# Retention kernel: the last projection further behind its heads, the work of a head spread out, and sample states stored from SyncE

## The chip, the cores and the metric

One core of a Trainium2 chip runs the whole program. The metric is the device time of one execution in microseconds (us). TensorE multiplies, VectorE (DVE) and ScalarE (ACT) work element by element, GpSimd (POOL) does a few operations, and SyncE (SP) issues most of the DMA transfers; ScalarE issues the rest. Each engine takes its instructions strictly in the order of the program, and the engines wait for each other on semaphores.

## What is computed

One inference step of a two-layer decoder for 512 prompt tokens and 8 x 8 sample tokens, 576 in all, in float32. Layer 0 is differential attention; the change starts where it ends. Layer 1 is multi-scale retention:

```python
for layer in range(DEPTH):
    ...
        hp = rms_norm(y_prompt, norm_pre_ret)
        hs = rms_norm(y_sample, norm_pre_ret)
        qp, kp, vp, gp = ret_project(hp, w_in_ret, pos_prompt)      # 2048 -> 12288
        op, sp = retention_prompt(qp, kp, vp, log_g)                # chunks of 128 tokens, 8 heads
        ss, osm = retention_chunk(state_ret, qs, ks_, vs, log_g)    # 8 samples, state (256, 512) per head
        y_prompt = y_prompt + rms_norm(ret_output(op, gp, w_out_ret), norm_post_ret)
        ret_state_sample = ss
...
def ret_output(o, g, w_out):
    on = head_rms_norm(o)...
    return (on * jax.nn.silu(g)) @ w_out                            # 4096 -> 2048
```

The states of the samples are read and written: 8 samples x 8 heads x 512 KB each way.

## The kernel before

The kernel is a list of stages in one order, written by a planner at build time; each engine goes through the whole list and does its share of each stage. The clock of the list is the **tile** (a **slot**): one `project` stage, six matmuls of 128x288. A large matrix product in float32 is made of three products of halves: every operand is split into a high part (`WH`, `XH`, made by ScalarE's copy, L1531) and a residue (`WL`, `XL`, made by VectorE's subtraction, L1845 for weights and L1850 for tokens). A weight chunk of 512 KB (`WR`) serves eight tiles; at the third tile of each chunk the next one is split and the one three further on is loaded (`load_w`, L1100).

Behind layer 0 come three stages of the program.

*Between the layers* (`norm_between`): the norms, and beside them the first input projections of layer 1 as tiles. Four quarters of the tokens are put together again from `XH` and `XL` (`x_rec`, 128x2304 each, two on VectorE L2110 and two on GpSimd L2370), mixed (`x_mix`, L2116) and split (`x_mix_split`, L2121), for the products that follow.

*The products* (`layer_one_inputs`): 42 of the 48 column blocks (head, kind) of the input projection, each in seven products of half size (24 matmuls of 128x288 each) where plain tiles need 32 tiles of six. The results go to `retention_inputs` in memory.

*The last stage* (`layer_one`): it lays the retention of eight heads under a stream of tiles. `retention_work` gives each head a table of slots, 64 slots per head (`PER_HEAD`). The stream begins with the three column blocks of head 7 that are left (96 tiles, `FILL`), and then come eight **parts** of the output projection, 64 tiles each: part h multiplies the gated tokens of head h. So part h begins at slot 96 of head h's own count. A head's stages, by name:

- `load_v4`, `load_qk`, `load_g4`: its inputs; `natural` (`r`): transposes of the values through bank 7, copied by ScalarE; `rope`: four VectorE operations per input (L2137 to L2142).
- `rs_keys`, `pad_rows`, `rs_mask`, `rs_out`, `rs_state`: the samples. `rs_out` is 17 matmuls of 128x512 (34 records); `rs_state` adds the new keys to the eight states in four steps of four banks (4 to 7), each drained by VectorE (L2207).
- `ret_scores`, `ret_out`, `ret_state` for four chunks; `ret_rstd` and `ret_norm` (L2199); `gate`: transposes, multiplied by VectorE with the gate (L2220).
- `store_ret` writes the gated tokens to memory (`gated_retention`), `load_x` (L1106) reads them back into `XL`, and four `split_x` (ScalarE L1531, VectorE L1850) make them ready for the part.
- `load_state` and `store_state` move the eight states, 512 KB each. A load waits until the store of the same buffer (head before) has landed.

The order in which a head's stages stand around the next head's is set by that table alone:

```python
    def put(t, *s):
        at.setdefault(max(t, -PER_HEAD * h), []).extend(s)
```

`store_state` waits for banks 4 to 7 to be drained and is issued by ScalarE (L1749). `load_x` waits for the stores of the gated tokens and for the matmuls before it.

## Time and profile before

| | before |
|---|---|
| median of 3 runs | 3733.25 us (3732.2 to 3734.78) |
| profiled execution | 3740.97 us, its span 3739.0 us |
| TensorE busy | 3418.2 us, 91% |
| VectorE busy | 2207.4 us, 59% |
| ScalarE busy | 1097.9 us, 29% |
| GpSimd busy | 87.4 us, 2% |
| read and written | 593.36 MB and 98.96 MB |

By the trace the stage between the layers lies from about 1600 to 1768 us, the products from there to about 2700 us, and the last stage from there to the end. Busy shares are means over stages with different limits; a matmul in the records is pipelined, so that a busy TensorE can still be one at half its clock. The row PEclk and the column PEclk give the clock that was granted.

### The profile page before, as it was taken

How to read it: one execution, taken by the hardware profiler on the slowest of the kernel's cores; microseconds unless marked ns; L12 is line 12 of the kernel's file. 1: busy time of each engine (PE TensorE's matmuls, PEld its weight loads, DVE VectorE, ACT ScalarE, POOL GpSimd, SP SyncE). 2: the span in 40 equal slices, each digit the busy share in tenths (PEclk: the TensorE clock that was granted, in tenths of full speed). 3: DMA queues.
4: the chain of work that ended last, by engine and by line, in shares of the span. 5: the costliest groups of instructions: out<-in, count | busy, mean ns of one | idle time of the engine just before them, and what ended most of it. 6: DMA issues, size and time to landing. Idle time of an engine off the chain costs nothing.

```text
span 3739.0 us, 65337 instructions
## 1 busy us (share of the span) xinstructions
PE 3418.2 (91%) x25236; PEld 3003.2 (80%) x25236; DVE 2207.4 (59%) x3329; ACT 1097.9 (29%) x1604; POOL 87.4 (2%) x89
## 2 busy tenths in 40 slices
PE   7999999999999998888999999999988778887787
PEld 7988887788788776778999999999976656666567
DVE  4466656565656664375777767777643455545555
ACT  4223222222222322143333333333323311222213
POOL 1000000000000000030000000000000000000000
PEclk9999999999999998999999999999999989998899
DMA  5466887788788877534333333333345554455534
GB/s 176 155 209 214 273 283 254 262 287 278 243 281 273 276 261 243 184 130 138 116 116 129 126 122 116 116 131 124 126 155 204 180 187 149 142 182 177 181 121 147
DMA packets 497127, 698.18 MB, mean 187 GB/s; under 512 B 37042, under 2 KB 295219, under 8 KB 493683
## 3 DMA queue, kind: packets, MB, share of 16 engines
q1 hardware_dynamic: 419010, 593.18, 48.0%
q10 hardware_dynamic: 77392, 100.55, 7.7%
q8 instruction: 201, 3.29, 0.4%
q0 software_dynamic: 416, 0.28, 0.1%
q14 instruction: 108, 0.88, 0.1%
HBM read 593.36 MB, written 98.96 MB: 185 GB/s over the span
## 4 chain that ended last, share of the span: by engine, by line
PE 76%; DVE 10%; DMA 5%; issue 3%; ACT 3%; SPq 1%; ACTq 0%; DVEq 0%; POOL 0%; POOLq 0%
PE low_banks L1227 49%; PE high_banks L1227 25%; DMA XL<-gated_retention 3%; PE high_banks L1230 2%; DVE area L2207 2%; DVE WL L1845 2%; DMA area<-in_cache_v 1%; ACT WH L1531 1%; DVE x_rows L1867 1%; DVE area L1941 1%; SPq L1132 1%; DVE area L2142 1%; ACT area L1531 0%; DVE area L2140 0%; DVE XL L1850 0%
## 5 line engine op out<-in xcount | busy, mean ns | idle before, releaser
L1227 PE MATMUL low_banks<-XH,WH 128*128 128x288 f32 (+2 forms) x4528 | 1127.9, 316 | 134.7 <-DVE XL L1850 87.8
L1227 PE MATMUL low_banks<-XH,WL 128*128 128x288 f32 (+2 forms) x4528 | 1055.0, 300 | 0.0
L1227 PE MATMUL low_banks<-XL,WH 128*128 128x288 f32 (+2 forms) x4528 | 1053.7, 299 | 0.0
L1227 PEld LDWEIGHTS low_banks<-XH,WH 128*128 128x128 f32 x4528 | 766.2, 193 | 298.2 <-issue 166.3
L1227 PEld LDWEIGHTS low_banks<-XL,WH 128*128 128x128 f32 x4528 | 769.3, 193 | 0.0
L1227 PEld LDWEIGHTS low_banks<-XH,WL 128*128 128x128 f32 x4528 | 768.6, 193 | 0.0
L1227 PE MATMUL high_banks<-area 128*32 128x256 f32 (+9 forms) x4720 | 650.2, 477 | 57.3 <-DVE area L2220 16.3
L1227 PEld LDWEIGHTS high_banks<-area 128*32 128x32 f32 (+3 forms) x4720 | 279.3, 142 | 277.1 <-issue 204.4
L1845 DVE TENSOR_TENSOR WL<-WR,WH 128x1024 fp32r<-128x1024 f32 x266 | 330.3, 1242 | 283.2 <-ACT WH L1531 277.9
L1531 ACT ACTIVATE WH<-WR 128x1024 fp32r<-128x1024 f32 x266 | 280.8, 1056 | 544.2 <-PE low_banks L1227 400.3
L1941 DVE STREAM_TRANSPOSE area<-area 128x512 f32<-128x512 f32 x512 | 334.7, 691 | 106.6 <-PE high_banks L1227 63.9
L1531 ACT ACTIVATE area<-high_banks 128x512 f32<-128x512 f32 (+2 forms) x224 | 118.7, 535 | 819.8 <-PE high_banks L1230 482.0
L2081 DVE TENSOR_TENSOR WL<-area,WH 128x1024 fp32r<-128x1024 f32 x196 | 240.2, 1226 | 154.0 <-ACT WH L1531 151.6
L1531 ACT ACTIVATE WH<-area 128x1024 fp32r<-128x1024 f32 x196 | 208.5, 1064 | 267.2 <-DVE area L2075 163.6
L1230 PE MATMUL high_banks<-eye_sb,area 128*128 128x128 f32 (+2 forms) x984 | 162.2, 286 | 104.6 <-DVE area L2199 45.0
L2075 DVE TENSOR_TENSOR area<-area 128x1024 f32<-128x1024 f32 x168 | 205.9, 1226 | 23.8 <-DVE third L2081 1.0
L1230 PEld LDWEIGHTS high_banks<-eye_sb,area 128*128 128x128 f32 (+2 forms) x984 | 117.3, 145 | 127.6 <-issue 63.5
L1227 PE MATMUL low_banks<-mixes,WH 128*128 128x288 f32 x896 | 178.9, 294 | 0.0
L1227 PE MATMUL high_banks<-mixes,WH 128*128 128x288 f32 x896 | 178.9, 294 | 0.0
L2081 DVE TENSOR_TENSOR third<-area,third 128x1024 fp32r<-128x1024 f32 x98 | 120.1, 1226 | 93.6 <-ACT third L1531 92.7
L1531 ACT ACTIVATE third<-area 128x1024 fp32r<-128x1024 f32 x98 | 104.3, 1064 | 158.3 <-DVE area L2075 83.1
L1227 PEld LDWEIGHTS low_banks<-mixes,WH 128*128 128x128 f32 x896 | 144.6, 189 | 0.0
(178 smaller groups left out, 3153.1 us busy)
## 6 DMA issues: line engine op xcount, KB each, us to landing
area<-in_cache_k SPq DMA_DIRECT2D x512, 256.0 KB, 4.6
area<-in_cache_v SPq DMA_DIRECT2D x512, 256.0 KB, 5.2
area<-in_w_in_ret SPq DMA_DIRECT2D x168, 512.0 KB, 5.8
WR<-in_w_in_attn SPq DMA_DIRECT2D x136, 512.0 KB, 5.3
out<-area ACTq DMA_DIRECT2D x73, 512.0 KB, 4.0
WR<-in_w_out_ret SPq DMA_DIRECT2D x66, 512.0 KB, 3.5
area<-in_state_ret SPq DMA_DIRECT2D x64, 512.0 KB, 10.8
retention_inputs<-area ACTq DMA_DIRECT2D x48, 576.0 KB, 2.9
```

Of the source, the lines that this page charges most:

```text
L1132: sp.dma_start(Vr[t:128:GROUP, half * GROUP:(half + 1) * GROUP, :], cv[page, :, pair * 512:(pair + 1) * 512].rearrange("a (o j) n -> j (a ...
L1227: return nc.tensor.matmul(out, a, b, start=start, stop=stop, skip_group_check=True)
L1230: return nc.tensor.matmul(out, a, ident[0:n, 0:n], start=True, stop=True, is_transpose=True, skip_group_check=True)
L1531: return nc.scalar.activation(out, in_, ACT.Copy, scale=scale)
L1845: v.tensor_tensor(WL[:, slot, :, :], WR[:, slot, :, :], WH[:, slot, :, :].bitcast(f32), SUB).then_inc(sem["w_lo"], 1)
L1867: last = v.tensor_tensor(dst[:, lo:hi], bank[2 * cb + b][:, 0:hi - lo], dst[:, lo:hi], ADD)
L1941: v.transpose(KTs[:, :, 128 * (u % 2) + 32 * pp:128 * (u % 2) + 32 * pp + 32], Kr[:, slot, :].rearrange("p (m i) -> p m i", i=32)).then_in ...
L2075: v.tensor_tensor(to, a, b, op).then_inc(sem["quad_sums"], 1)
L2081: v.tensor_tensor(lo, quad(r, what), hi.bitcast(f32), SUB).then_inc(sem["w_lo"], 1)
L2142: v.tensor_tensor(mine[:], mine[:], rt[:], ADD).then_inc(sem["rotated"], 1)
L2207: v.scalar_tensor_tensor(out=mine, in0=mine, scalar=decay8[:, g:g + 1], in1=bank[4 + j][:, :], op0=MUL, op1=ADD).then_inc(sem[f"drained{4 ...
```

## The change

It has five parts.

1. *Distance.* `FILL` goes from 96 to 128 and every head's table moves by `BASE` = 8. Part h now begins 120 slots behind the start of head h's table, where it was 96. The 32 tiles that fill the gap are two column blocks that leave the products: (0,3) goes to the stage between the layers and (7,2) to the last stage (40 blocks remain in the products, and 656 tiles stand in the last stage where there were 624).
2. *Spread.* Within a head's table `load_x` goes from slot 72 to 84 and `split_x` from 78, 80, 82, 84 to 105, 109, 113, 117; `load_state` from every 2 slots at 6 to every 3 at 22 (slots of the next head); `rs_out` from 49 to 56; `rs_state` from 56, 59, 62, 65 to 65, 69, 73, 77; the gates from 52, 55, 58, 61, 64 to 54, 57, 60, 63, 67.
3. *Stores.* `store_state` is issued by SyncE, two slots apart from slot 73 on (61 before).
4. *Between the layers.* All four `x_rec` go to GpSimd, one behind the other; the mixes and their splits go in halves of 128x1152 into slots 133 to 191, where the tiles of (0,2) and (0,3) run.
5. *Slots of weights.* The products' ring begins at slot 0, and the first weight chunk of the last stage is loaded into `spare_chunk`, the room of the products' `first_sum`, one product earlier than before.

```diff
-FILL = 96
+FILL = 128
 PER_HEAD = 64
+BASE = 8
...
     def put(t, *s):
-        at.setdefault(max(t, -PER_HEAD * h), []).extend(s)
+        at.setdefault(max(BASE + t, -PER_HEAD * h), []).extend(s)
...
-            put(6 + 2 * k + (2 if k > 3 else 0), Stage("load_state", b=2 * (k % 4) + k // 4))
+            put(22 + 3 * k, Stage("load_state", b=2 * (k % 4) + k // 4))
...
-        put(52 + 3 * t, Stage("gate", t=t))
-        put(54 + 3 * t, Stage("store_ret", t=t))
...
+        put(54 + 3 * t, Stage("gate", t=t))
+        put(57 + 3 * t, Stage("store_ret", t=t))
+    put(56, Stage("rs_out"))
...
-            put(56 + 3 * (2 * g + e), Stage("rs_state", g_=g, e=e))
+            put(65 + 4 * (2 * g + e), Stage("rs_state", g_=g, e=e))
         for j in range(4):
-            put(61 + 7 * g + 2 * j, Stage("store_state", b=2 * j + g))
-    if h < HEADS:
-        kt = CH * (h % 2)
-        put(72, Stage("load_x", part=h % 2, kt=kt, row=CH * h, width=T, layer=1))
-        for k in range(CH):
-            put(78 + 2 * k, Stage("split_x", part=h % 2, kt=kt + k, width=T))
+            put(73 + 8 * g + 2 * j, Stage("store_state", b=2 * j + g))
+    kt = CH * (h % 2)
+    put(96 if h == 0 else 84, Stage("load_x", part=h % 2, kt=kt, row=CH * h, width=T, layer=1))
+    for k in range(CH):
+        put(105 + 4 * k, Stage("split_x", part=h % 2, kt=kt + k, width=T))
...
-          24: lambda: n.scale(4), 25: lambda: rec((0, 0), 2, "pool"), 26: lambda: rec((1, 0), 4, "pool"),
-          36: lambda: n.transpose(4), 40: lambda: rec((1, 1), 3, "dve"), 46: lambda: rec((0, 1), 1, "dve"), 52: lambda: mix(3),
...
+          24: lambda: n.scale(4), 36: lambda: n.transpose(4), 40: lambda: rec((0, 0), 2) + rec((1, 0), 4) + rec((1, 1), 3) + rec((0, 1), 1),
...
-    order = [(n, (n, lo, hi)) for lo, hi in ((0, EARLY), (EARLY, T)) for n in range(2)] + [(2, None)]
+    order = [(n, (n, lo, hi)) for lo, hi in ((0, EARLY), (EARLY, T)) for n in range(2)] + [(2, None), (3, None)]
...
-    for s in range(3, 6):
+    for s in range(2, 6):
...
-    todo = [(h, s) for h in range(HEADS) for s in range(6)][3:-3]
+    todo = [(h, s) for h in range(HEADS) for s in range(6)][4:-4]
...
+            def store_state(g, b):
+                for n in range(4, 8):
+                    sp.wait_ge(sem[f"drained{n}"], c.before(f"drained{n}"))
+                sp.dma_start(st_out[g + b * HEADS], Sin[:, b, :].rearrange("p (e v) -> p e v", e=2)).then_inc(sem[f"state_out{b}"], 16)
```

In the order of the changed program line numbers are a few off: L1103 is `load_w`, L1109 `load_x`, L1202 `load_state`, L1207 `store_state`, L1195 `load_g4`, L1188 `load_v4`, L1235 a matmul and L1238 a transpose, L1849 the subtraction for `WL`, L2286 that for `XL` in the norm, L2111 a mix and L2365 a sum on GpSimd.

**SyncE, from one head's `load_g4` to the loads of the next head's states.** Before:

```order
L1199 DMA area<-in_state_ret 128x2x512
L1192 DMA area<-retention_inputs 128x4x576
L1106 DMA XL<-gated_retention 128x4x576
L1199 DMA area<-in_state_ret 128x2x512 x2
L1100 DMA WR<-in_w_out_ret 128x4x256
L1199 DMA area<-in_state_ret 128x2x512 x3
```

Of the change:

```order
L1207 DMA out<-area 128x2x512
L1195 DMA area<-retention_inputs 128x4x576
L1103 DMA WR<-in_w_out_ret 128x4x256
L1207 DMA out<-area 128x2x512 x4
L1103 DMA WR<-in_w_out_ret 128x4x256
L1207 DMA out<-area 128x2x512
L1109 DMA XL<-gated_retention 128x4x576
L1207 DMA out<-area 128x2x512
L1202 DMA area<-in_state_ret 128x2x512
L1207 DMA out<-area 128x2x512
L1188 DMA area<-retention_inputs 128x4x576
L1202 DMA area<-in_state_ret 128x2x512
```

The load of `XL` stood among the loads of states; it now stands ahead of them, behind six stores.

**TensorE, at the third `rs_state` of a head.** Before, after two tiles of the projection, the transposes of the last gate and of the first `natural` follow (x8):

```order
L1227 MATMUL high_banks<-area 128x512 x4
L1227 MATMUL low_banks<-XH,WH 128x288 x2
L1227 MATMUL low_banks<-XL,WH 128x288 x2
L1227 MATMUL low_banks<-XH,WL 128x288 x2
...
L1230 MATMUL high_banks<-eye_sb,area 128x128 x8
```

Of the change, at the second and the fourth `rs_state`:

```order
L1235 MATMUL high_banks<-area 128x512 x4
L1238 MATMUL high_banks<-eye_sb,area 128x128 x4
L1235 MATMUL low_banks<-XH,WH 128x288 x2
...
L1235 MATMUL high_banks<-area 128x512 x4
L1235 MATMUL high_banks<-area 64x64 x2
L1238 MATMUL high_banks<-eye_sb,area 64x128 x2
```

A `natural` of the next head (`eye_sb`, 128x128) now stands directly behind the second `rs_state` (and one behind the third), and the matmuls of `rs_keys` (64x64) behind the fourth, with no tile between.

**VectorE, between the layers.** Before (L1845 is `WL`, L2110 a sum, L2116 a mix, L2290 the residues of the last tokens):

```order
L1845 TENSOR_TENSOR WL<-WR,WH 128x1024 x2
L2290 TENSOR_TENSOR XL<-high_banks,XH 128x4x64 x4
L2110 TENSOR_TENSOR area<-XH,XL 128x2304
L1845 TENSOR_TENSOR WL<-WR,WH 128x1024
L2110 TENSOR_TENSOR area<-XH,XL 128x2304
L1845 TENSOR_TENSOR WL<-WR,WH 128x1024
L2116 TENSOR_TENSOR area<-area 128x2304 x2
```

Of the change:

```order
L1849 TENSOR_TENSOR WL<-WR,WH 128x1024 x2
L2286 TENSOR_TENSOR XL<-high_banks,XH 128x4x64 x4
L1849 TENSOR_TENSOR WL<-WR,WH 128x1024 x12
L2111 TENSOR_TENSOR area<-area 128x1152 x2
```

The sums have left VectorE; twelve weight subtractions now follow one another before the first mix. On GpSimd the two sums are four.

## Rows read from the trace of the kernel before

**Rows 1.** The page, busy tenths and granted clock in 40 slices of the span.

```profile
PE   7999999999999998888999999999988778887787
...
PEclk9999999999999998999999999999999989998899
```

**Rows 2.** Stages: us, busy of PE, PEld, DVE, ACT, POOL; PEclk, DMA share, GB/s.

```profile
2400.00:2600.00 200.00, 200.00 (x1514) 200.00 (x1513) 141.93 (x144) 73.83 (x81) 0.00 (x0) 1.00 0.36 122
3050.60:3166.40 115.80, 93.11 (x555) 72.45 (x554) 60.51 (x98) 24.42 (x39) 2.62 (x2) 0.90 0.49 167
```

**Rows 3.** TensorE's waits, 2690 to 3739: us in total, times, longest.

```profile
PE low_banks L1227 <- DVE XL L1850: 79.0, 8, 10.7
PE high_banks L1230 <- DVE area L2199: 45.0, 24, 2.9
PE high_banks L1230 <- DVE area L2207: 22.1, 19, 2.0
PE high_banks L1227 <- DVE area L2220: 16.3, 21, 1.6
PE high_banks L1230 <- ACT area L1531: 9.9, 6, 6.7
PE high_banks L1227 <- DVE area L2161: 5.5, 8, 1.1
PE high_banks L1227 <- ACT area L1531: 5.4, 7, 1.7
```

**Rows 4.** The chain that ended last: start, us, what (longest and shortest of eight).

```profile
3398.04 15.58 DMA XL<-gated_retention
...
3618.26 11.98 DMA XL<-gated_retention
```

**Rows 5.** Timeline of one head: start, us, engine, line, operation, idle before.

```profile
3050.65 0.46 SPq L1106 DMA_DIRECT2D XL<-gated_retention  x1
...
3065.47 0.68 ACT L1531 ACTIVATE XH<-XL 128x576 fp32r<-128x576 f32 x1 [10.95 <-DMA XL<-gated_retention]
...
3069.04 0.85 PE L1227 MATMUL low_banks<-XH,WH 128*128 128x288 f32 x2 [10.23 <-DVE XL L1850]
...
3069.69 0.68 PE L1227 MATMUL low_banks<-XL,WH 128*128 128x288 f32 x2
...
3076.49 0.42 PE L1227 MATMUL low_banks<-XL,WH 128*128 128x288 f32 x2
```

**Rows 6.** The chain in the products stage: start, us, what.

```profile
1813.08 25.39 PE low_banks L1227 x192
```

**Rows 7.** DMA issues, 2830 to 3500: count, size, median us to landing.

```profile
WR<-in_w_out_ret SPq DMA_DIRECT2D x47, 512.0 KB, 3.5
...
area<-in_state_ret SPq DMA_DIRECT2D x45, 512.0 KB, 10.9
...
XL<-gated_retention SPq DMA_DIRECT2D x5, 1152.0 KB, 15.3
```

**Rows 8.** Timeline of the same head, from `rs_out` to the last `rs_state`.

```profile
3115.82 4.70 PE L1227 MATMUL high_banks<-area 64*128 64x512 f32 x34
...
3122.88 1.23 DVE L1845 TENSOR_TENSOR WL<-WR,WH 128x1024 fp32r<-128x1024 f32 x1 [6.28 <-ACT WH L1531]
...
3124.68 0.66 PE L1230 MATMUL high_banks<-eye_sb,area 128*128 128x128 f32 x4 [1.58 <-DVE area L2199]
...
3155.84 2.72 DVE L2207 SCALAR_TENSOR_TENSOR area<-area,high_banks 128x512 f32<-128x512 f32 x4 [1.81 <-PE high_banks L1227]
...
3158.71 0.63 PE L1230 MATMUL high_banks<-eye_sb,area 128*128 128x128 f32 x4 [1.97 <-DVE area L2207]
```

**Rows 9.** Between the layers: TensorE's waits for `WL`; timeline of GpSimd and VectorE.

```profile
PE low_banks L1227 <- DVE WL L1845: 23.1, 6, 6.0
...
1669.01 13.10 POOL L2370 TENSOR_TENSOR area<-XH,XL 128x2304 f32<-128x2304 f32 x2 [3.94 <-DVE XL L2290]
...
1671.10 12.09 DVE L1845 TENSOR_TENSOR WL<-WR,WH 128x1024 fp32r<-128x1024 f32 x2
```

More of the change, by code:

```diff
@@ L512, in split @@
         n, i = divmod(m, 7)
-        self.splits[m] = Stage("quad_split", r=n % 2, what=PRODUCTS[i], slot=(m + 2) % 3, summed=self.sums.get((n, PRODUCTS[i])))
+        self.splits[m] = Stage("quad_split", r=n % 2, what=PRODUCTS[i], slot=m % 3, summed=self.sums.get((n, PRODUCTS[i])))
         out = [self.splits[m]]
@@ L547, in layer_one_inputs @@
     for m in range(prods.count):
-        out += prods.split(m + 2) + prods.product(m) + after.get(prods.count - m, [])
+        out += (prods.split(m + 2) if m else []) + prods.product(m) + after.get(prods.count - m, [])
     return out + prods.store(len(prods.pairs) - 1)
@@ L577, in retention_work @@
             put(5 * hh + 2 * j, Stage("natural", what="r", hh=hh, j=j))
-    put(7, loads["g"])
-    put(20, Stage("silu_g"))
-    put(12, Stage("rs_keys"))
-    put(13, Stage("pad_rows"))
-    put(21, Stage("rs_mask"))
-    for c in range(4):
-        put(14 + 9 * c, Stage("ret_scores", c=c))
-        put(17 + 9 * c, Stage("ret_out", c=c))
-        put(18 + 9 * c, Stage("ret_state", c=c))
-    put(48, Stage("store_state_p"))
-    put(47, Stage("ret_rstd", t=0, n=4))
-    put(49, Stage("rs_out"))
@@ L590, in retention_work @@
-    put(54, Stage("ret_rstd", t=4, n=1))
-    for t in range(4):
-        put(50 + t, Stage("ret_norm", t=t))
-        put(52 + 3 * t, Stage("gate", t=t))
-        put(54 + 3 * t, Stage("store_ret", t=t))
-    put(57, Stage("ret_norm", t=4))
-    put(64, Stage("gate", t=4))
-    put(66, Stage("store_ret", t=4))
+    put(10, loads["g"])
+    put(24, Stage("silu_g"))
+    put(13, Stage("rs_keys"))
+    put(14, Stage("pad_rows"))
+    put(22, Stage("rs_mask"))
+    for c in range(4):
+        put(15 + 9 * c, Stage("ret_scores", c=c))
+        put(18 + 9 * c, Stage("ret_out", c=c))
+        put(19 + 9 * c, Stage("ret_state", c=c))
@@ L810, in plan @@
     stored = Stored(proj, prods, last)
-    begun = last.load(0) + last.load(1)
-    for x in begun:
-        x.a["behind_products"] = True
-    opening = {9: [Stage("load_rope")], 3: begun}
+    begun = last.load(0), last.load(1)
+    begun[0][0].a["spare"] = begun[1][0].a["behind_products"] = True
+    opening = {9: [Stage("load_rope")], 4: begun[0], 2: begun[1]}
     inputs = layer_one_inputs(prods, opening)
@@ L819, in plan @@
     at = inputs.index(prods.mm[prods.count - 1])
-    inputs[at:at] = [Stage("split_w", slot=0)] + last.load(2)
+    inputs[at:at] = [Stage("split_w", slot=1, spare=True)] + last.load(2)
     inputs += [Stage("relay_area"), Stage("pads"), Stage("load_head")] + [Stage("load_state", b=2 * (k % 4) + k // 4) for k in range(8)]
```

102 lines of the change are left out of this document (52 added, 50 removed).

## The prediction

> **What bounds the kernel now.** I began with the page's slices: TensorE is the engine that the time is made of, and in the last third its digit drops from 9 to 7 or 8 while its granted clock drops too [rows 1]. The table by stages says how much. In 200 us of the products stage TensorE is busy for all 200 us at clock 1.00; in one head of the last stage (115.8 us) it is busy for 93.1 us at clock 0.90 [rows 2]. A reader should see that an edit in the products stage could at best trade one TensorE instruction for another, and that some 25 us of each head are there to be won. So I asked for TensorE's waits from 2690 us to the end [rows 3]: 79.0 us in 8 waits are for `XL` (the residues of the gated tokens that a part multiplies), 45.0 us for `ret_norm` on VectorE (L2199), and 22.1 + 16.3 + 9.9 + 5.4 + 5.5 = 59.2 us for banks and operands that VectorE or ScalarE had still to drain or make.
>
> The chain shows what stands behind the 79 us: a load of `gated_retention` once per head, from 12.0 to 15.6 us each, eight of them [rows 4]. The timeline of one head has the story in order [rows 5]: SyncE issues the load at 3050.65; ScalarE, which takes its work in order, sits 10.95 us at the first `split_x`; VectorE follows; TensorE stands until 3069.04. After that its pairs of matmuls take 0.68 us and not 0.42, until about 3075.8, a little before the last row of the group. That is 6.8 us at the half clock (1.2 GHz), so 3.4 us lost on top of every 10 us wait.
>
> **Extra work.** Columns (0,3) and (7,2) leave the seven products and are computed tile by tile: 192 matmuls in place of 168, twice, at 25.39/192 = 0.132 us [rows 6]: **+6.3 us**. One tile (6 matmuls, a slot) is 0.79 us. Nothing hides this; TensorE is full there.
>
> **The load of XL.** Before, it is put at slot 72 of its head, its first split at 78 and the part at 96. Now they are at 84, 105 and 120 after the head's own start (each 8 later in the program's count). The load takes 15.3 us to land [rows 7]; 21 slots are 16.7 us of projection alone, and two chunks of retention lie between. It is also issued before the eight state loads rather than among them. The last split (slot 117) has 3 slots, 2.4 us, and the 4.7 us of `rs_out` [rows 8] in front of its user, against 0.68 us of work on ScalarE [rows 5] and about as much on VectorE. I take all 79 us and the 8 x 3.4 us: **-106 us**. Bounds: -40 (half of each wait returns, and the clock with it) and -106.
>
> **Gates.** Today `rs_out` and the weight split stand before three of the four `ret_norm`s on VectorE: it idles 6.28 us for `WH`, and the gate waits 1.58 us [rows 8]. Now `rs_out` comes 7 slots later, behind the norms. But `rope` and now a `split_x` lie among the norms, so I keep one wait of 2.5 us per head (between today's mean, 1.9, and longest, 2.9): 45 becomes 20, **-25 us**. Bounds 0 and -45.
>
> **Banks.** Here the change costs. `rs_state` moves from slots 56, 59, 62, 65 to 65, 69, 73, 77, straight into the next head's `natural` (64, 66, 68, 69, 71, 73, all bank 7) and `rs_keys` (77). VectorE drains an `rs_state` in 2.72 us, bank 7 last; the one natural that stands a slot behind one today waits 1.97 us [rows 8]. Per head: natural behind gate 3 on bank 7, 1.6 (today's longest L2220 wait [rows 3]); natural 66, 2.0; naturals 69 and 73 with no slot between, 2.7 and 2.3; `rs_keys` 0.8 until bank 4 is free; `ret_scores` 0 two slots later needs bank 4 again, after 2.72 and the operations of `rs_keys` ahead of it, the largest on 1024 elements like a `WL` (1.23, [rows 8]), 2.1; ScalarE's drains 1.0. That is 12.5 us, and for seven heads and a rest of 4 us some 91 us, against 52.5 us today (59.2 less the 6.7 us of the start). **+39 us**, and **+5 us** for more time at the half clock in so broken a stretch. Bounds: 0, and +112 (TensorE and VectorE take turns wholly, about 20 us per head).
>
> **Between the layers.** The four half-size sums of `XH` and `XL` now all go to GpSimd, and the eight mixes to slots where nothing is short. Today two sums on GpSimd take 13.10 us, 6.55 each, and in that time VectorE's two `WL` subtractions take 12.09 us instead of 1.23 each; TensorE waits 23.1 us for `WL` in this stage [rows 9]. Four sums are 26.2 us, one `WL` getting in after each, while a chunk of 24 matmuls lasts at most 3.2 us: 26.2 - 4 x 3.2 = 13.4 us of waiting in place of 23.1. VectorE has no sums or mixes in its way meanwhile. **-10 us**, between +5 (no `WL` gets in between) and -20 (the load of `WR` that now lies behind eight loads of `quads` is hidden as well, and the clock holds).
>
> The Trainium skill (SBUF — State Buffer, section SBUF: two separate sides) says that a GpSimd operation and a VectorE operation with two SBUF inputs exclude each other for a whole instruction. The trace agrees: 12.09 us for two. By that rule alone four sums block twice as long as two do, which speaks against this edit: some 0 us where I subtract 10 (rival 6).
>
> **The start of the last stage.** TensorE stands 6.7 us at the first `natural` (the longest L1531 wait of [rows 3]), since ScalarE waits for the stores of the products. With 8 slots ahead of it TensorE works on, then misses its second weight chunk: **-3 us**, bounds 0 and -6.7.
>
> **The stores of the states.** 64 issues leave ScalarE for SyncE. Their landing costs the same there; behind each wait for drained banks now stand weight loads. A weight load has 16 slots, 12.7 us, and lands in 3.5 us [rows 7], so 9 us are spare. ScalarE, busy for 24.4 of 115.8 us [rows 2], is short of nothing but its place in the order. **0**; the bounds are those of rivals 2 and 4.
>
> **Sum.** +6.3 - 106 - 25 + 39 + 5 - 10 - 3 = -93.7 us. The profiled execution took 3740.97 us (span 3739.0), so 3647; the median of the runs is 7.7 us below it, so **3640 us**.
>
> **Rivals.**
> 1. *More is won (3600).* The bank waits stay as they are today: VectorE is busy for 60.5 of 115.8 us [rows 2], not full. Then +39 and +5 fall away. Against: two naturals follow `rs_state` with nothing between. 0.17.
> 2. *The XL wait only shrinks (3690).* Eight state stores of 512 KB each now go into the queue that carries the load, six of them issued just before it. If it lands 10 us later than today, about half of the 106 us stay. For: today it takes 15.3 us and a state 10.9 us in this same queue, against 3.5 us for a weight chunk [rows 7]. Against: it is no longer behind state loads. 0.14. The Trainium skill (DMA: Bandwidth & Descriptors, section Queues, rings and completion order) says that each DMA engine takes turns between the rings of the issuing engines; with ScalarE's ring empty the loads lose nothing to it, but wait their turn behind the stores in their own. No row here has stores in SyncE's queue at this place.
> 3. *Banks cost more (3700).* 20 us per head. TensorE and VectorE then take turns. For: in the 16 slots from 63 to 79 VectorE has 4 x 2.72 us of drains, two `WL` and by my estimate 6 to 7 us besides, some 20 us, and TensorE as much. Against: today the two overlap all but 2 us of each drain. 0.12.
> 4. *Slower (3745).* SyncE holds at a store until VectorE has drained `rs_state`, and the weight loads behind it come late. Three such loads per head stand among the stores, 24 in all. Each must come 9 + 4 us late to eat the 94 us. SyncE's place in the program is never far ahead of TensorE today either, as every weight load waits for `w_lo`. 0.04.
> 5. *Nothing moves (3733).* The wait for XL goes over whole to another in-order wait of ScalarE, such as `silu_g` for its load. 0.03.
> 6. *The GpSimd sums run back to back (3650).* No `WL` gets in between, and one waits for all 26.2 us; TensorE has one chunk in hand, 3.2 us, and stands 23 us, as today. For: the four are now one run in GpSimd's order. Against: between today's two one `WL` did get in, as each took 6 us [rows 9]. 0.05.
>
> My forecast has 0.45.
>
> **Range.** All good bounds together give 3562, all bad ones 3778. 8 in 10 lie within 3600 to 3695, from rival 1 to just short of 3. 0.2% (7.5 us) is about what a measurement tells from no change: faster 0.92, same 0.04, slower 0.04.
>
> **What would show it.** TensorE's waits for `XL` in the last stage near 0 and the clock above 0.95; a head every 102 to 105 us instead of 116; the L2199 waits at half or less; waits for the successor of L2207 up from 22 to 60 us or more. Four GpSimd sums of about 6.5 us between the layers, with `WL` at 6 us beside them. I am wrong if waits for `WL` appear in the last stage (rival 4), or if ScalarE idles for the load of XL again (rival 2).

## The result, and the profile after

| | before | changed |
|---|---|---|
| median | 3734.02 us (3732.2 to 3735.65, 4 runs) | 3673.99 us (3665.89 to 3681.93, 4 runs) |
| profiled execution, its span | 3740.97 us, 3739.0 us | 3670.28 us, 3668.5 us |
| TensorE, VectorE, ScalarE busy | 91%, 59%, 29% | 93%, 60%, 30% |

The ratio is 0.9839, with a 95% interval from 0.9815 to 0.9863: 60 us faster by the medians, where 94 were forecast. 3640 was given, with a range of 3600 to 3695.

The page of the changed kernel, the same two rows as [rows 1]:

```profile
PE   7999999999999998888999999999988888888897
...
PEclk9999999999999999999999999999999989999999
```

The last third is now 8 up to its last two slices (9 and 7), where it was 7 and 8. It isn't the 9 of the products stage. The stage table, one head of the last stage (as the second row of [rows 2]):

```profile
3142.00:3249.40 107.40, 89.62 (x558) 71.75 (x557) 60.94 (x99) 24.44 (x39) 3.05 (x2) 0.95 0.53 182
```

A head takes 107.4 us where it took 115.8, at clock 0.95 instead of 0.90. I had forecast 102 to 105, and a clock above 0.95. TensorE's waits from 2650 us to the end answer to [rows 3]. L2203 is VectorE's drain of `rs_state` (L2207 before), L2195 the norms (L2199), L2216 the gates (L2220), L2157 `rs_keys` (L2161):

```profile
PE high_banks L1238 <- DVE area L2203: 55.6, 29, 3.3
PE high_banks L1238 <- DVE area L2195: 21.9, 8, 3.6
PE high_banks L1238 <- DVE area L2216: 14.8, 7, 2.4
PE high_banks L1235 <- issue: 12.5, 10, 2.2
PE low_banks L1235 <- DVE WL L1849: 11.7, 4, 5.3
PE high_banks L1235 <- DVE area L2157: 11.5, 8, 3.8
PE high_banks L1235 <- DVE area L2203: 7.1, 7, 1.0
...
PE high_banks L1235 <- DVE area L2216: 4.0, 5, 1.9
```

`XL` is gone from the list, from 79.0 us. The norms went from 45.0 to 21.9. The successors of `rs_state` rose from 22.1 to 62.7. One entry was not in the forecast at all: 12.5 us under "issue", which had been 0.9.

**Who holds TensorE under "issue".** The timeline of one head, at the start of the next head's retention:

```profile
3236.98 0.51 ACTq L1727 DMA_DIRECT2D area<-area  x1
...
3243.02 0.48 ACT L1539 ACTIVATE area<-high_banks,area 128x256 f32<-128x256 f32 x1 [6.44 <-issue]
...
3243.59 1.10 PE L1235 MATMUL high_banks<-area 128*128 128x512 f32 x2 [1.56 <-issue]
```

From 3236.98 to 3243.0 ScalarE issues the eight small transfers of `pad_rows`. Only then does it drain the bank of the first `ret_scores` (3243.02), for which `ret_out` has waited 1.56 us. Issuing a transfer isn't counted as an engine's work in this profile, so the view names no engine and calls the wait "issue".

**The gate.** The timeline at the first gate:

```profile
3182.13 0.76 DVE L2133 SCALAR_TENSOR_TENSOR area<-area 128x576 f32<-128x576 f32 x1
3182.92 0.76 DVE L2134 TENSOR_TENSOR area<-area 128x576 f32<-128x576 f32 x1
3183.71 0.95 DVE L1871 TENSOR_TENSOR x_rows<-low_banks,x_rows 128x288 f32<-128x288 f32 x2
3184.70 0.76 DVE L1854 TENSOR_TENSOR XL<-XL,XH 128x576 fp32r<-128x576 f32 x1
3185.49 0.49 DVE L2195 TENSOR_SCALAR area<-area 128x512 f32<-128x512 f32 x1
...
3186.03 0.66 PE L1238 MATMUL high_banks<-eye_sb,area 128*128 128x128 f32 x4 [3.57 <-DVE area L2195]
...
3188.05 0.68 PE L1235 MATMUL low_banks<-XL,WH 128*128 128x288 f32 x2
```

Before the third norm (3185.49) VectorE does two rotations, a tile's drain and the residue of a `split_x`. The gate waits for that norm 3.57 us, and behind it the pairs of matmuls take 0.68 us instead of 0.42, as they did behind the `XL` wait [rows 5]. The half clock didn't leave with that wait. There are shorter pieces of it behind three of the head's waits (3.57, 1.98 and 2.98 us). The wait of 1.98 us ends 5.6 us behind one of 2.40; a second wait of 2.98 us, at 3219.57, has no such piece behind it:

```profile
3184.00:3190.00 6.00, 3.97 (x17) 3.33 (x18) 4.88 (x9) 0.00 (x0) 0.00 (x0) 0.75 0.04 13
3208.00:3214.00 6.00, 4.02 (x22) 3.80 (x21) 3.58 (x6) 1.54 (x2) 0.00 (x0) 0.74 0.15 46
3226.00:3232.00 6.00, 4.13 (x20) 4.15 (x21) 2.95 (x4) 1.32 (x2) 0.00 (x0) 0.72 0.30 83
```

The last column but two is the granted clock. In slices of 6 us the rest of the head was at 1.00, but for two at 0.97. The kernel before had such pieces too, beside the one behind the wait for `XL`. In the head of [rows 5] they lie behind waits of 1.84 and 2.91 us for norms:

```profile
3128.00:3134.00 6.00, 4.42 (x21) 2.93 (x22) 4.56 (x10) 0.00 (x0) 1.59 (x1) 0.72 0.02 6
3140.00:3146.00 6.00, 5.25 (x21) 3.69 (x22) 4.70 (x7) 0.00 (x0) 0.00 (x0) 0.51 0.27 88
```

**DMA issues**, 2830 to 3500, median us to landing in the last column (as [rows 7]):

```profile
out<-area SPq DMA_DIRECT2D x48, 512.0 KB, 5.9
...
XL<-gated_retention SPq DMA_DIRECT2D x7, 1152.0 KB, 8.2
```

The load of `XL` lands in 8.2 us instead of 15.3. Six stores stand ahead of it in its own queue, but in the head of the timelines SyncE issued five of them 5 to 26 us before it (3222.95 to 3243.9, the load at 3249.44), and only the sixth at 3248.93.

**Between the layers** (as [rows 9]), the wait for `WL`, the four sums and VectorE beside them:

```profile
PE low_banks L1235 <- DVE WL L1849: 17.9, 7, 5.3
...
1668.88 23.30 POOL L2365 TENSOR_TENSOR area<-XH,XL 128x2304 f32<-128x2304 f32 x4 [11.47 <-DVE XL L2286]
...
1670.36 16.84 DVE L1849 TENSOR_TENSOR WL<-WR,WH 128x1024 fp32r<-128x1024 f32 x3 [1.56 <-ACT WH L1539]
1687.75 5.52 DVE L1849 TENSOR_TENSOR WL<-WR,WH 128x1024 fp32r<-128x1024 f32 x1 [0.54 <-ACT WH L1539]
```

### The profile page after: what moved, and what is told of

It is laid out like the page before. It is cut to its first block, busy times and chain, and to the rows that moved or that the text cites. A ratio compares the mean times of both kernels' runs of the same rounds, so it can differ in the third digit from the quotient of the medians.

```text
span 3668.5 us, 65373 instructions
## 1 busy us (share of the span) xinstructions
PE 3396.9 (93%) x25284; PEld 2998.6 (82%) x25284; DVE 2190.2 (60%) x3311; ACT 1094.4 (30%) x1606; POOL 100.2 (3%) x91
## 4 chain that ended last, share of the span: by engine, by line
PE 79%; DVE 10%; issue 3%; DMA 3%; ACT 2%; SPq 1%; DVEq 0%; POOL 0%; ACTq 0%; POOLq 0%
PE low_banks L1235 52%; PE high_banks L1235 25%; PE high_banks L1238 2%; DVE WL L1849 2%; DVE area L2203 2%; DMA area<-in_cache_v 1%; ACT WH L1539 1%; SPq L1135 1%; DVE area L1945 1%; DVE x_rows L1871 1%; DMA WR<-in_w_in_ret 1%; DMA area<-in_cache_k 0%; DVE XL L2286 0%; ACT XH L1539 0%; DVE area L2134 0%
## 5 line engine op out<-in xcount | busy, mean ns | idle before, releaser
L1235 PE MATMUL low_banks<-XH,WH 128*128 128x288 f32 (+2 forms) x4632 | 1141.3, 314 | 60.8 <-DVE WL L1849 33.4
L1235 PE MATMUL low_banks<-XH,WL 128*128 128x288 f32 (+2 forms) x4632 | 1073.8, 299 | 0.0
L1235 PE MATMUL low_banks<-XL,WH 128*128 128x288 f32 (+2 forms) x4632 | 1073.2, 299 | 0.0
L1235 PEld LDWEIGHTS low_banks<-XH,WH 128*128 128x128 f32 x4632 | 781.0, 193 | 197.4 <-issue 140.6
L1235 PEld LDWEIGHTS low_banks<-XL,WH 128*128 128x128 f32 x4632 | 784.0, 193 | 0.0
L1235 PEld LDWEIGHTS low_banks<-XH,WL 128*128 128x128 f32 x4632 | 783.5, 192 | 0.0
L1235 PE MATMUL high_banks<-area 128*32 128x256 f32 (+9 forms) x4720 | 637.5, 470 | 66.6 <-DMA area<-in_cache_v 14.9
L1235 PEld LDWEIGHTS high_banks<-area 128*32 128x32 f32 (+3 forms) x4720 | 273.7, 139 | 292.8 <-issue 211.4
L1849 DVE TENSOR_TENSOR WL<-WR,WH 128x1024 fp32r<-128x1024 f32 x273 | 346.8, 1270 | 269.3 <-ACT WH L1539 263.3
L1238 PE MATMUL high_banks<-eye_sb,area 128*128 128x128 f32 (+2 forms) x984 | 160.7, 284 | 120.1 <-DVE area L2203 55.6
L1238 PEld LDWEIGHTS high_banks<-eye_sb,area 128*128 128x128 f32 (+2 forms) x984 | 118.3, 144 | 147.1 <-issue 108.6
L1235 PE MATMUL high_banks<-mixes,WH 128*128 128x288 f32 x864 | 172.6, 294 | 0.0
L1235 PE MATMUL low_banks<-mixes,WH 128*128 128x288 f32 x848 | 169.4, 294 | 0.0
L2319 POOL TENSOR_TENSOR area<-area,power 128x1 f32<-128x1 f32 (+4 forms) x67 | 52.9, 790 | 3518.1 <-DVE area L1820 3099.6
L1596 ACT ACTIVATE area<-low_banks 128x288 f32<-128x288 f32 (+2 forms) x192 | 79.0, 412 | 224.9 <-PE low_banks L1235 216.5
```

Of the source, the lines that this page charges most:

```text
L1235: return nc.tensor.matmul(out, a, b, start=start, stop=stop, skip_group_check=True)
L1238: return nc.tensor.matmul(out, a, ident[0:n, 0:n], start=True, stop=True, is_transpose=True, skip_group_check=True)
L1596: last = nc.scalar.activation(dst[:, lo:hi], bank[2 * cb + b][:, 0:hi - lo], f)
L1849: v.tensor_tensor(WL[:, slot, :, :], spare_chunk if spare else WR[:, slot, :, :], WH[:, slot, :, :].bitcast(f32), SUB).then_inc(sem["w_lo" ...
L2319: nc.gpsimd.tensor_tensor(out, a, power[0:R, 0:n], ALU.pow).then_inc(sem[name], 1)
```

## The experiments

Each edit is against the changed kernel unless it says otherwise. All were timed in five rounds beside the kernel before, whose median was 3734.65, 3732.83, 3732.82 and 3737.27 us in the four groups (one to four, five to eight, nine to eleven, twelve).

| | median us | ratio to before, 95% |
|---|---|---|
| e1 before, stores by SyncE | 3728.35 | 0.9983 [0.9974, 0.9992] |
| e2 changed, stores by ScalarE | 3676.85 | 0.9852 [0.9837, 0.9867] |
| e3 distance alone | 3651.76 | 0.9782 [0.9769, 0.9795] |
| e4 between the layers as before | 3681.78 | 0.9863 [0.9847, 0.9878] |
| e5 gates new, states old | 3673.72 | 0.9843 [0.9824, 0.9863] |
| e6 states new, gates old | 3693.32 | 0.9891 [0.9872, 0.9910] |
| e7 `pad_rows` later | 3714.67 | 0.9947 [0.9931, 0.9964] |
| e8 first states later | 3676.82 | 0.9846 [0.9829, 0.9863] |
| e9 naturals between | 3623.88 | 0.9705 [0.9692, 0.9718] |
| e10 norms early | 3658.35 | 0.9810 [0.9796, 0.9823] |
| e11 distance, `rs_out` later | 3618.64 | 0.9691 [0.9677, 0.9704] |
| e12 e9 and e10 | 3605.64 | 0.9648 [0.9626, 0.9671] |

**Experiments 1 and 2: who issues the stores.** The first is the kernel before with `store_state` moved to SyncE, at its old slots; the second the changed kernel with it moved back.

```diff
-                    act.wait_ge(sem[f"drained{n}"], c.before(f"drained{n}"))
-                act.dma_start(st_out[g + b * HEADS], Sin[:, b, :].rearrange("p (e v) -> p e v", e=2)).then_inc(sem[f"state_out{b}"], 16)
+                    sp.wait_ge(sem[f"drained{n}"], c.before(f"drained{n}"))
+                sp.dma_start(st_out[g + b * HEADS], Sin[:, b, :].rearrange("p (e v) -> p e v", e=2)).then_inc(sem[f"state_out{b}"], 16)
```

> The kernel before with nothing changed but who issues the stores of the sample states (SyncE in place of ScalarE). Theory A (the issuer is off the path): 3734 within 8 us, the eight waits for XL stay near 79 us in total and the load of XL lands in about 15 us. Theory B (SyncE's queue is what the stores harm): the load of XL lands in over 18 us, its waits grow above 90 us and the time is 3745 or more. Theory C (ScalarE was held by the stores' waits and is now free): the waits for XL shrink and the time is 3720 or less.

> The changed kernel with the stores of the states issued by ScalarE again. Theory A: as the changed kernel, 3674 within 10 us, no wait for XL. Theory B: faster than the changed kernel by 10 us or more, since the loads no longer stand behind stores. Theory C: slower by 10 us or more, since ScalarE stands at each store until VectorE has drained rs_state, and copies and weight splits behind it come late.

Measured: 6 us less than before, and 3 us more than the changed kernel, inside its scatter. The longest entry in the waits of the first:

```profile
PE low_banks L1232 <- DVE XL L1850: 86.9, 8, 12.1
```

The wait for `XL` grew by 8 us (79.0 before), as it would with SyncE held at stores, although the load itself lands sooner (12.5 us for 15.3); `WL` stays as it was (4.3, and 4.0 before). The waits for ScalarE's drains fell from 15.3 [rows 3] to 8.6. Rival 4's mechanism is worth a few us, if that is what the 8 us are, and didn't reach the weight loads. The stores land later from SyncE: 5.9 us in the changed kernel, and 3.5 in experiment 2. The Trainium skill (DMA: Bandwidth & Descriptors, section Queues, rings and completion order) has the DMA engines take turns between the rings of the issuing engines. The 3.5 and 5.9 agree with it, since stores in a ring of their own get turns of their own. The prediction had their landing cost the same. The time doesn't follow them: only the load of the same buffer waits for a store, and it stands 13 slots (10 us) or more behind it.

**Experiment 3: distance alone.** The changed kernel with the head's table of before and stores by ScalarE. The later part, the load and splits of `XL` at their new slots, the stage between the layers and the spare chunk stay as changed.

```diff
-            put(22 + 3 * k, Stage("load_state", ...
+            put(6 + 2 * k + (2 if k > 3 else 0), Stage("load_state", ...
...
-    put(56, Stage("rs_out"))
+    put(49, Stage("rs_out"))
...
-        put(54 + 3 * t, Stage("gate", t=t))
+        put(52 + 3 * t, Stage("gate", t=t))
...
-            put(65 + 4 * (2 * g + e), Stage("rs_state", g_=g, e=e))
+            put(56 + 3 * (2 * g + e), Stage("rs_state", g_=g, e=e))
```

> The distance alone: FILL 128, BASE 8, the two columns moved, load_x at 84 and split_x from 105 on, and everything between the layers as in the changed kernel; the other slots of a head (state loads, rs_out, gates, rs_state) as in the kernel before, stores by ScalarE. Theory A (the waits add up, and the spread traded gate waits for bank waits): no wait for XL, L2199-type waits near 45 us, bank waits near 52 us, so about as fast as the changed kernel or faster: 3640 to 3675. Theory B (the spread is what lets the load of XL land in time): waits for XL of 30 us or more in total come back, and the time is above 3690.

Measured: 3651.8 us, **faster than the whole change by 22**. Its waits:

```profile
PE high_banks L1234 <- DVE area L2196: 48.3, 24, 2.9
PE high_banks L1234 <- DVE area L2204: 20.7, 18, 2.0
PE high_banks L1231 <- DVE area L2217: 16.0, 20, 1.6
...
PE high_banks L1231 <- issue: 7.6, 7, 1.7
```

No `XL` wait either, so the distance, with the load and the splits at their new slots, takes it away without the stores and without the rest of the spread. The norms stay at 48.3 and the banks near what they were. So the rest of the spread as a whole loses: it takes 26 us off the norms, and adds 43 at the banks (50.2 to 93.0) and 5 under "issue" (7.6 to 12.5).

**Experiment 4: between the layers as before** (two sums on each engine, whole mixes, in their old slots).

> The changed kernel with the sums and mixes between the layers as in the kernel before (two sums on GpSimd at slots 25 and 26, two on VectorE at 40 and 46, whole mixes from slot 52 on). Theory A (my forecast, 10 us of gain there): 7 to 12 us slower than the changed kernel, with some 23 us of waits for WL in that stage in place of 18. Theory B (the four sums in a row on GpSimd cost what they save): the same time within 3 us.

Measured: 3681.8 us, 8 more than changed. The intervals of the two ratios overlap, but the stage itself settles it: it is 170.6 us long where it is 161.3 in the changed kernel. TensorE's wait for `WL` there is back:

```profile
PE low_banks L1234 <- DVE WL L1847: 23.0, 7, 5.7
```

**Experiments 5 and 6: the square.** Distance alone has both gates and states old, the changed kernel both new. These have one of each.

Experiment 5, against the changed kernel:

```diff
-            put(65 + 4 * (2 * g + e), Stage("rs_state", g_=g, e=e))
+            put(56 + 3 * (2 * g + e), Stage("rs_state", g_=g, e=e))
...
-            put(73 + 8 * g + 2 * j, Stage("store_state", b=2 * j + g))
+            put(61 + 7 * g + 2 * j, Stage("store_state", b=2 * j + g))
```

Experiment 6, against distance alone, has the same lines the other way, and:

```diff
-            put(6 + 2 * k + (2 if k > 3 else 0), Stage("load_state", ...
+            put(22 + 3 * k, Stage("load_state", ...
```

> The changed kernel, but with rs_state back at slots 56, 59, 62, 65 and its stores at 61 and on (rs_out 56, norms and gates as changed). With the other three kernels it makes a square: distance alone (gates and states old) took 3651.8 us, the changed kernel (both new) 3674. Theory A (the move of the states costs, the move of rs_out and the gates gains): the waits on TensorE for L2203's successor fall from 55.6 + 7.1 to some 25 us, those for the norms stay near 22 instead of 48.3, and the time is 3625 to 3640 us. Theory B (rs_state now stands directly behind rs_out and among the gates, and the gates' own drains stand behind its four 0.68 us operations on VectorE): nothing is won over distance alone, 3645 to 3665. Theory C (the states' place costs nothing, something else in the spread does): 3665 or more.

> Distance alone (3651.8 us), plus rs_state at 65, 69, 73, 77, its stores (by ScalarE) from 73 and the state loads at 22 and on; rs_out and gates at their old slots. Theory A (the states' move alone costs what the prediction took for banks, +39 and +5 for the clock): 3685 to 3700 us, with the norms' waits still near 48 and the banks' near 93. Theory C (the states' place is not it): 3645 to 3660. In between, 3665 to 3680, would say that the gates' new slots brought nothing, and the move of the states costs the 22 us by itself.

Measured: 3673.7 and 3693.3 us. For the first theory A fell. The number lies in the range of theory C, but the waits show B's mechanism, at 22 us over distance alone where B allowed 13. The second is where theory A had it, though by other waits than it named. The waits of experiment 5:

```profile
PE high_banks L1238 <- DVE area L2203: 68.0, 32, 2.8
...
PE high_banks L1235 <- ACT area L1736: 13.9, 8, 1.8
```

and of experiment 6:

```profile
PE high_banks L1234 <- DVE area L2204: 55.7, 21, 3.0
PE high_banks L1234 <- DVE area L2196: 35.9, 23, 2.6
PE high_banks L1231 <- issue: 29.4, 7, 4.2
```

In experiment 5 the norms' waits fall to 21.9 as foreseen, but each gate now stands a slot or less behind an `rs_state` (gates 57, 60, 63 behind 56, 59, 62) and waits until bank 7 or 6 is drained: 68.0 us against 20.7. In distance alone the same two kinds of stages alternate with the gate a slot *ahead* of the `rs_state`. Also `rs_state` now stands directly behind `rs_out` and waits 13.9 us for ScalarE to drain bank 6. In experiment 6 the naturals behind `rs_state` wait as in the changed kernel (55.7), the norms less than expected (35.9), and the wait at `pad_rows` is 4.2 us a head. There the last `rs_state` stands behind `rs_keys`, one slot ahead of the first scores, and `pad_rows` waits until VectorE has drained it: in the head of the timeline that drain runs from 3363.33 to 3366.05, and ScalarE, idle since 3362.45, issues its first transfer at 3366.16. In the changed kernel the drain ends at 3236.87 and the issues begin at 3236.98, but `rs_keys` and one slot more lie between that `rs_state` and `ret_out`. That this makes it 4.2 and not 1.6 is read from the order, not tried. So the price isn't that of moving the states, or the gates. It is mainly that of a bank's user directly behind the `rs_state` that fills four banks, wherever the two meet.

**Experiment 7: `pad_rows` later.**

```diff
-    put(14, Stage("pad_rows"))
-    put(22, Stage("rs_mask"))
+    put(20, Stage("pad_rows"))
+    put(31, Stage("rs_mask"))
```

> The changed kernel with pad_rows at slot 20 instead of 14 and rs_mask at 31 instead of 22, so that ScalarE drains the first scores before it issues the eight small transfers. Theory A (the 12.5 us that the waits of TensorE book under issue are mostly ret_out held by these issues, 1.6 us per head): the time falls by 8 to 14 us against the changed kernel, to 3660 to 3666. Theory B (the issues push the scores of the second chunk back by as much): within 4 us of the changed kernel, about 3670 to 3677.

Measured: 3714.7 us, **41 more**, outside of both theories. The timeline shows the eight issues in their new place:

```profile
3393.12 0.59 ACTq L1727 DMA_DIRECT2D area<-area  x1
...
3398.06 0.68 ACTq L1728 DMA_DIRECT2D area<-area  x1
...
3398.87 2.12 ACT L1639 ACTIVATE area<-area 128x2304 f32<-128x2304 f32 x1 [8.48 <-issue]
3400.89 0.46 ACT L1539 ACTIVATE area<-high_banks,area 128x256 f32<-128x256 f32 x1
...
3401.45 5.46 PE L1235 MATMUL high_banks<-area 128*128 128x512 f32 x6 [3.89 <-issue]
```

They take 5.6 us, about as in the old place (6.0), but now `silu_g` (2.12 us) follows, then the drain of the second scores and the weight split. `ret_out` waits 3.89 us and its chunk is done at the half clock (5.46 us for six matmuls that take 2.74 in the changed kernel). Ahead of the issues ScalarE stands idle from 3390.4 to 3393.12, since `pad_rows` now also waits for VectorE's copy of the first `ret_state`, which ends at 3393.04. In the first three heads ScalarE still drains the tiles' banks, and there tiles wait instead, 4.1, 7.0 and 5.0 us (the first two in this entry):

```profile
PE low_banks L1235 <- ACT area L1596: 11.1, 2, 7.0
```

All waits together grow by 26 us (148.8 to 174.4, 10 of them under "issue", 16 in these three), and the stage by 40; the rest lies outside the waits, as the half clock does. The old place was the cheaper one. I read the 12.5 us rightly as `pad_rows`, and was wrong that a later slot ends them.

**Experiment 8: the first head's states loaded later.**

```diff
-    inputs += [..., Stage("load_head")] + [Stage("load_state", b=2 * (k % 4) + k // 4) for k in range(8)]
+    inputs += [..., Stage("load_head")]
...
-            put(22 + 3 * k, Stage("load_state", ...
+        put(22 + 3 * k if h else 12 + 3 * k, Stage("load_state", ...
```

> The changed kernel with the eight state loads of the first head moved from before the last stage into it (slots 12 to 33 of that head, three apart). Theory A (the 11.7 us that TensorE waits for WL in this stage are weight loads queued behind eight state loads at its start): WL waits of the last stage fall to 6 us or less, and the time by 4 to 8 us, to 3666 to 3670. Theory B (the relay's wait for the stores of the products is the limit): WL waits stay at 10 or more and the time is within 3 us of the changed kernel's.

Measured: 3676.8 us, no gain, as theory B had it (the last stage alone is 2.0 us shorter). One wait of 3.8 us for `rs_keys` went, but the `WL` waits stay:

```profile
PE low_banks L1235 <- DVE WL L1849: 10.1, 4, 5.1
```

Half of it is one wait of about 5 us at the start, for the second chunk: it comes as ScalarE stands behind the last stores of the products, whose landing took 6.0 us in the chain of the changed kernel, with 2 us more until ScalarE went on. The state loads had a part in the 3.8 us alone.

**Experiments 9 and 10: the naturals between, the norms early.** The naturals of heads 1 to 7 go one slot ahead of an `rs_state` of the head before where they stood directly behind it; separately, the four norms go to one slot, ahead of the rotations and of `split_x`.

```diff
-            put(5 * hh + 2 * j, Stage("natural", what="r", hh=hh, j=j))
+            put((-3, 0, 4, 8, 16, 12)[3 * hh + j] if h else 5 * hh + 2 * j, Stage("natural", what="r", hh=hh, j=j))
```

```diff
-        put(51 + t, Stage("ret_norm", t=t))
+        put(51, Stage("ret_norm", t=t))
```

> The changed kernel with the six naturals of heads 1 to 7 put one slot or more ahead of each rs_state of the head before (61, 64, 68, 72, 76, 80 of its slots) instead of directly behind them. Theory A (the +39 us of the prediction are the place of a bank user directly behind a four-bank drain): TensorE's waits for L2203's successors fall from 62.7 to 30 us or less, and the time by 25 to 45 us, to 3630 to 3650. Theory B (VectorE's drains are the limit in this stretch whatever stands behind them, so the wait moves to the next bank user or to rs_state itself): the waits keep their sum, and the time stays within 10 us of the changed kernel's 3674.

> The changed kernel with the four ret_norms all at slot 51 instead of 51 to 54, so that VectorE does them ahead of the rotation's and split_x's operations. Theory A (the 3.57 us wait of the first gate is the third norm standing behind these, and the half clock behind it costs some 2 us more): the waits for L2195 fall from 21.9 to 8 us or less, and the time by 12 to 30 us, to 3645 to 3662. Theory B (the clock falls anyway, and the operations put behind are waited for by another): within 8 us of 3674.

Measured: 3623.9 us, 50 less than changed, and 3658.4 us, 16 less. The waits of experiment 9:

```profile
PE high_banks L1235 <- DVE area L2216: 13.4, 8, 2.2
PE high_banks L1235 <- ACT area L1539: 12.3, 8, 2.2
...
PE high_banks L1238 <- DVE area L2203: 7.2, 21, 0.5
...
PE high_banks L1235 <- issue: 3.7, 3, 2.2
```

and of experiment 10:

```profile
PE high_banks L1235 <- DVE area L2216: 13.3, 13, 1.9
...
PE high_banks L1238 <- DVE area L2195: 4.5, 6, 1.5
```

The 55.6 us behind `rs_state` are 7.2: the drain of four banks is as long as it was (2.72 us), and TensorE does tiles in that time. Two other waits grew. An `rs_state` now stands behind the drain of a gate (13.4 us, 4.0 in the changed kernel). `ret_out`, which waited under "issue" for `pad_rows`, now waits for the copy of a natural that ScalarE does behind it (12.3 us and 3.7 under "issue", where it was 0 and 12.5). Together they are a smaller price. The time went below the 3630 to 3650 of theory A.

The norms' 21.9 us are 4.5 in experiment 10. Of the 17.4 us that went, 9.3 came back at `rs_out`, which now waits for a gate's drain (4.0 to 13.3): a part of theory B.

In both the time fell by more than the waits did. All waits from 2650 us on sum to 148.8 us in the changed kernel, 109.9 in experiment 9 and 138.3 in experiment 10, so 38.9 and 10.5 less. The last stage, from its first tile to the end, is 999.2, 951.7 and 979.5 us, so 47.4 and 19.6 less. The rest, 8.5 and 9.1 us, lies outside the waits, where the half clock is. That it is the clock isn't certain: in experiments 2 and 4, with the last stage of the changed kernel but for who issues the stores, what is left of the stage without its waits is 5.7 and 2.8 us less than there.

**Experiment 11: distance alone, with `rs_out` later** and the norms in one slot (against distance alone; the samples' `ret_rstd` goes from 54 to 56 and their norm from 57 to 59).

```diff
-    put(49, Stage("rs_out"))
...
+    put(54, Stage("rs_out"))
...
-        put(50 + t, Stage("ret_norm", t=t))
+        put(50, Stage("ret_norm", t=t))
```

> Distance alone (3651.8 us) with the four norms together at slot 50 and rs_out at 54 instead of 49 (the norm of the samples at 59). Theory A (the 48.3 us of waits for the norms are rs_out and the weight split that waits behind it on ScalarE): those waits fall to 15 us or less and the time by 25 to 40 us, to 3612 to 3627. Theory B (as in the kernel with the gates moved and the states in place, what the gates win the banks take back, since rs_state now stands two slots behind rs_out and must wait for its bank): 3645 to 3660.

Measured: 3618.6 us, 33 less than distance alone, as theory A had it:

```profile
PE high_banks L1234 <- DVE area L2196: 4.6, 6, 1.5
```

The norms' waits fall from 48.3 to 4.6 while the states stay where they were; the matmuls' waits for a gate's drain rise from 16.0 to 31.1. Which of the two moves did it, `rs_out` or the norms, isn't separated.

**Experiment 12: both edits of 9 and 10.**

> The changed kernel with both edits together: the naturals ahead of each rs_state (alone 3623.9 us against 3674) and the four norms at slot 51 (alone 3658.4). Theory A (the two waits are separate, each with its own half-clock stretch behind it): the gains add, 50 and 16, and the time is 3600 to 3616 us, below both the changed kernel and distance alone, with waits for L2203's successors near 14 and for L2195 near 5 us. Theory B (one covers the other, since both shorten the same stretch of TensorE and VectorE then becomes the limit): 3617 to 3627.

Measured: 3605.6 us, **the fastest of all**, 3.5% below before and some 68 us below the changed kernel, for 50 + 16 from the two alone. One head of it:

```profile
3108.96:3207.74 98.78, 88.36 (x559) 70.00 (x558) 60.70 (x99) 24.43 (x40) 3.05 (x2) 0.97 0.57 197
```

## Why the prediction was right, and what it missed

Its range held the time and the forecast case came true in the main, but it forecast 94 us where 60 came. The terms, by the profiled executions:

| term | forecast | measured | from |
|---|---|---|---|
| extra matmuls | +6.3 | +6.3 | count; the products stage is 44.4 us shorter, and 2 x 7 x 24 x 0.132 = 44.4 |
| wait for `XL` | -79 | -79 | 79.0 to 0 |
| clock | -22 | -12.5 | the rest, below |
| gates | -25 | -23.1 | 45.0 to 21.9 |
| banks | +39 | +37 | 52.5 to 89.2 (93.0 less 3.8 of the start) |
| `pad_rows` | 0 | +11.6 | "issue", 0.9 to 12.5 |
| between the layers | -10 | -7.2 | below |
| start of the last stage | -3 | +3.5 | 6.7 to 6.4 (`WL`) + 3.8 (`rs_keys`) |
| other waits | 0 | +0.7 | `WL` at the end 4.0 to 5.3, norms of the output 10.3 to 9.7 |

They sum to -63 us; the clock is what the others leave of the last stage, so the sum is no check of it. The last stage and the stage between the layers are in it, but not the attention, which ended 7.6 us earlier in this profiled execution than in that of before (1617.68 instead of 1625.27 us for the first operation behind it). With these it is the 70.5 us by which the spans differ. It is scatter: in experiment 8 the last stage began 9.4 us later than in the changed kernel, with nothing changed ahead of it. The medians put the change at 60.

**The load of XL** was right in full, and experiment 3 shows that the distance, with the new slots of the load and its splits, does it. It even landed sooner (8.2 for 15.3 us). That it would suffer behind the stores (rival 2) fell, and its premise too: of the six stores one was issued just before it. Before, it stood among the eight state loads (slots 70 to 86, itself at 72), and SyncE had issued `load_g4`, another 1152 KB, 0.77 us ahead of it. In experiment 3 it comes behind most state loads, in the changed kernel ahead; `load_g4` is 17 and 20 us ahead; and it lands in 8.2 us in both. Which of these neighbours held it no run separates.

**The clock was the term that was mis-sized.** I priced the half clock as a thing that belongs to the wait for `XL`: 8 x 3.4 us, less 5. Waits of 2 to 4 us cost some too. Three per head do here, and two did in the kernel before, which I had not looked for. In the last stage the waits fell from 198.4 to 148.8 us and the stage from 1035.8 to 999.15, with 25.4 us of work added. That is (1035.8 - 198.4 + 25.4) - (999.15 - 148.8) = 12.5 us, put down to the clock. With the executions of experiments 1, 2 and 4 in place of one or both kernels it comes to 10 to 18 us, so it is short of the 22 but known only to some us.

**Gates.** The one wait of 2.5 us per head was 2.7 us on the mean (21.9 / 8), and its cause was the one named, rotations and a `split_x` among the norms. I had taken it as given; one line removes it (experiment 10), worth 16 us in all.

**Banks** were sized within 2 us, in part by luck: in one head the gate (2.4 for 1.6) and the last natural (2.98 for 2.3) cost more than listed, and `ret_scores` (1.1 for 2.1) and ScalarE's drains (none for 1.0) less. This term is what makes the whole change slower than its own first part. The prediction had the order in hand ("naturals 69 and 73 with no slot between, 2.7 and 2.3"; measured 2.98 each) and so could have said that the spread loses. It added the terms up instead of asking whether each part pays: -25 for the gates and +39 + 5 for the banks is +19, and +22 was measured, 5 of them at `pad_rows`. That was in my sum, and I left it unsaid. Rival 1 (banks cost nothing) is what experiment 9 made true by another order.

**`pad_rows`** is the step that failed. I wrote that ScalarE "is short of nothing but its place in the order", and then priced that place at 0; it cost 11.6 us. Most of that came with the distance: experiment 3, with the `rs_state`s and the naturals at their old slots, has 7.6 of the 12.5 us. The kernel before has the same run of issues in the same place, but there TensorE stood for `XL` meanwhile:

```profile
3059.00 0.61 ACTq L1719 DMA_DIRECT2D area<-area  x1
...
3066.18 0.48 ACT L1531 ACTIVATE area<-high_banks,area 128x256 f32<-128x256 f32 x1
```

The last issue ends at 3059.6, the first scores are drained at 3066.18, and TensorE, held for `XL` until 3069.04, comes to `ret_out` after that. Take the long wait away, and the short one beneath it shows. This is read from the order of the timelines; no run has the kernel before without its `XL` wait and nothing else changed. The 5 us more of the changed kernel came with the spread, by which the last `rs_state` stands just ahead of `pad_rows`, which waits for its drain.

**The start of the last stage.** My step was that TensorE misses only the second weight chunk. It does miss it, for 5.3 us, waits another 1.1 us for the first and 3.8 us for `rs_keys`, whose weight split stood behind a load of `WR` that lay behind the eight state loads (11.7 us to land). Experiment 8 took that last one away.

**Between the layers.** -7.2 us in the profile, and 8 by experiment 4 (9.3 by its stage). Four `WL` got in beside four sums, as forecast, at 5.6 and 5.5 us each. The Trainium skill (SBUF — State Buffer, section SBUF: two separate sides) has a GpSimd operation and a VectorE operation with two inputs in SBUF exclude each other for the whole instruction. By these rows it holds for each pair; back to back over all four (rival 6) it does not, as in the kernel before.

**The stores** were 0 to 6 us, in either direction: rival 4's mechanism, if the 8 us of experiment 1 are its, is tiny.

**The range.** By the prediction's own bounds all bad ones together are 3733 + 6.3 - 40 + 112 + 5 + 5, so 3822 and not 3778. The range of 3600 to 3695 and the chances don't rest on it.

## What to carry to other kernels

When an edit has several parts, work out the sign of each part and not only of the sum: here the distance gained 83 us (some 8 of them between the layers) and the spread gave 22 back. Before a long wait is taken away, look at what goes on beneath it: here that was worth 7.6 us. Where a stage fills several banks at once, the slots behind it belong to stages that need none of them; moving the next user ahead of it was worth 50 us at no cost in work. A run of DMA issues on a computing engine is work (0.6 us each), and before it is moved one has to look at what will stand behind it.

## What the runs showed of the hardware

- The half clock isn't the price of long waits only. In slices of 6 us at the end of waits of 3.57, 1.98 and 2.98 us the granted clock was 0.72 to 0.75, with pairs of matmuls at 0.68 us for 0.42. When the wait for `XL` had gone, about half of its clock loss was won (12.5 of 27 us, within the scatter above).
- How long a load takes to land hangs on its neighbours in the queue: the same 1152 KB took 15.3 us among loads of states and 0.77 us behind another 1152 KB, and 8.2 us in two other orders.
- Eight issues of small transfers on ScalarE took 5.6 to 6.0 us, and no engine is named for the wait behind them.
- Four sums on GpSimd took 23.3 us, 5.8 each, where I had 6.55 each from two. A `WL` beside them took 5.5 or 5.6 us instead of 1.23.
